# Products of the identity issued on TensorE ahead of its waits in the layer norms, the routing and the start of the feed-forward

## What is computed

```python
def first_block(...):
    for l in range(DEPTH):
        mix = hybrid_mixer(x, w_in[l], ...)
        x = layer_norm(ALPHA * x + mix, ln1_g[l], ln1_b[l])
        ffn = grouped_moe(x, router_w, router_bias, w_gate[l], w_up[l], w_down[l])
        x = layer_norm(ALPHA * x + ffn, ln2_g[l], ln2_b[l])
    return x

def second_block(x, ...):
    h = x
    for layer in range(DEPTH):
        mix = hgrn2_mixer(h, ...) if layer < N_A_LAYERS else swa_sink_mixer(h, k_shared, v_shared, ...)
        h = layer_norm_2(ALPHA_2 * h + mix, ln_mix_g[layer], ln_mix_b[layer])
        ff = conv_ffn(h, ffn_w_in[layer], ffn_conv_w[layer], ffn_conv_b[layer], ffn_w_out[layer])
        h = layer_norm_2(ALPHA_2 * h + ff, ln_ffn_g[layer], ln_ffn_b[layer])
        if layer == N_A_LAYERS - 1:
            k_flat, v_flat = jnp.split(h @ shared_w_kv, 2, axis=-1)
    return h
```

## Time and profile before

| | |
|---|---|
| median of three runs | 1679.57 us |
| the profiled execution | 1681.4 us |
| its span in the trace | 1679.6 us |
| TensorE busy | 1480.0 us |
| VectorE busy | 610.1 us |
| ScalarE busy | 463.4 us |
| GpSimd busy | 120.1 us |
| granted clock of TensorE, mean | 0.934 |

### The profile page before, as it was taken

How to read it: one execution, slowest core, us unless ns; L and a number is a source line. 1 busy time by engine, 2 the same in 40 slices (tenths; PEclk the granted TensorE clock), 3 DMA queues, 4 the chain that set the end, 5 groups by cost and what they waited for, 6 DMA issues and landing times.

```text
span 1679.6 us, 20234 instructions
## 1 busy us (share of the span) xinstructions
PE 1480.0 (88%) x7774; PEld 962.5 (57%) x7774; DVE 610.1 (36%) x1231; ACT 463.4 (28%) x866; POOL 120.1 (7%) x135
## 2 busy tenths in 40 slices
PE   6978699999699778999987897797999896899997
PEld 3854543433276444343426886367994384499943
DVE  0253311111213532011106597328770335477702
ACT  1251111110123412111104332044750035167500
POOL 1011000000000300000002151003000003000000
PEclk9999799999799889999997998869999898899999
DMA  9420499999916036999996421246564440255630
GB/s 328 152 100 1 159 392 394 397 392 393 334 52 248 1 128 224 397 392 393 397 383 199 153 89 63 83 153 195 171 232 145 136 171 1 87 189 172 228 125 25
DMA packets 184814, 347.45 MB, mean 207 GB/s; under 512 B 8208, under 2 KB 84262, under 8 KB 184628
## 3 DMA queue, kind: packets, MB, share of 16 engines
q1 hardware_dynamic: 179920, 330.19, 55.1%
q0 software_dynamic: 3968, 15.84, 2.6%
q10 hardware_dynamic: 868, 0.63, 0.1%
HBM read 342.44 MB, written 4.19 MB: 206 GB/s over the span
## 4 chain that ended last, share of the span: by engine, by line
PE 74%; SPq 9%; DVE 8%; DMA 3%; ACT 3%; issue 2%; POOL 0%; DVEq 0%; ACTq 0%
PE bank L1444 16%; SPq L575 9%; PE bank L1875 9%; PE bank L1643 8%; PE bank L1760 7%; PE bank L1761 7%; PE bank L1762 7%; PE bank L1653 5%; PE bank L1664 3%; PE bank L1704 3%; DMA slot<-in_w_down 2%; PE bank L1792 2%; PE bank L1886 1%; ACT arena L745 1%; DVE w_low L1363 1%
## 5 line engine op out<-in xcount | busy, mean ns | idle before, releaser
L1760 PE MATMUL bank<-x_high,w_high 128*128 128x256 f32 x912 | 264.0, 289 | 18.7 <-DVE w_low L1363 14.1
L1761 PE MATMUL bank<-x_low,w_high 128*128 128x256 f32 x912 | 262.9, 288 | 0.0
L1762 PE MATMUL bank<-x_high,w_low 128*128 128x256 f32 x912 | 262.7, 288 | 0.0
L1643 PE MATMUL bank<-slot,arena 128*64 128x512 f32 x1024 | 223.9, 594 | 1.6 <-DMA slot<-in_w_up 1.3
L708 ACT ACTIVATE arena<-bank 128x512 f32<-128x512 f32 (+7 forms) x196 | 99.3, 533 | 371.7 <-PE bank L1653 122.6
L1760 PEld LDWEIGHTS bank<-x_high,w_high 128*128 128x128 f32 x912 | 180.4, 198 | 20.2 <-DVE w_low L1363 14.8
L1761 PEld LDWEIGHTS bank<-x_low,w_high 128*128 128x128 f32 x912 | 180.3, 198 | 0.0
L1762 PEld LDWEIGHTS bank<-x_high,w_low 128*128 128x128 f32 x912 | 180.1, 197 | 0.0
L708 ACT ACTIVATE w_high<-slot 128x1024 fp32r<-128x1024 f32 x130 | 129.9, 1051 | 118.4 <-PE bank L1762 89.3
L1643 PEld LDWEIGHTS bank<-slot,arena 128*64 128x64 f32 x1024 | 72.4, 137 | 149.9 <-issue 149.9
L1875 PE MATMUL bank<-slot,arena 128*128 128x512 f32 x352 | 151.4, 592 | 0.0
(11 more groups left out here) (252 smaller groups left out, 1700.3 us busy)
## 6 DMA issues: line engine op xcount, KB each, us to landing
slot<-in_w_gate SPq DMA_DIRECT2D x64, 1024.0 KB, 14.0
slot<-in_w_up SPq DMA_DIRECT2D x64, 1024.0 KB, 14.2
slot<-in_w_down SPq DMA_DIRECT2D x64, 1024.0 KB, 13.9
slot<-in_ffn_w_in SPq DMA_DIRECT2D x44, 1024.0 KB, 7.5
slot<-in_ffn_w_out SPq DMA_DIRECT2D x22, 1024.0 KB, 5.0
slot<-in_hgrn_w_in SPq DMA_DIRECT2D x16, 1024.0 KB, 6.1
slot<-in_w_in SPq DMA_DIRECT2D x10, 1024.0 KB, 11.2
slot<-in_w_o SPq DMA_DIRECT2D x8, 1024.0 KB, 7.1
```

The lines of the kernel that those rows point to most:

```text
L1643: last = mm(banks_gu["gu".index(m)][rows, :], B["xe"][:, 4 * half + c, rows], ws[e][:, c, :], start=(half == 0 and c == 0), stop=(half == ...
L1760: mm(dst, high[:, k, :], x_high[:, k, :], start=(k == 0), stop=False)
L1761: mm(dst, high[:, k, :], x_low[:, k, :], start=False, stop=False)
L1762: last = mm(dst, low[:, k, :], x_high[:, k, :], start=False, stop=(k == KD - 1))
```

## The change

A function `busy(b, n)` issues n float32 products of the identity (128x128) with the identity repeated four times (128x512) into a bank. Nobody reads them, and no semaphore is raised. Each later job starts its bank anew. It is called

- in transpose_x for all calls but "in", ahead of the wait for the tile: 8 products ahead of tile 1, and ahead of tile 0 12 for the names "m" and "z", none for "y". `reuse` of the first bank comes ahead of them;
- in route ahead of the wait for `chosen_ready`: 8;
- in experts ahead of the wait for `slots_ready`: 7;
- in feed_forward ahead of the wait for the convolution's weights: 3, and behind their transposes, ahead of the first product: 5.

```diff
+            def busy(b, n):
+
+                for _ in range(n):
+                    mm(b[:, :], ident[:, :], ident[:, :].unsqueeze(1).to_broadcast([P, 4, P]), start=True, stop=True)
+
             def transpose_x(l, y, ready):
                 for t in range(NT):
+                    if y != "in":
+                        busy(reuse(pe, (l, f"{y}xT{t}0")), (8 if t else 12 if y in "mz" else 0))
                     ready(t)
...
                 b = reuse(pe, (l, "rank"))
+                busy(b, 8)
                 pe.wait_ge(sem("chosen_ready"), l + 1)
...
+                busy(reuse(pe, (l, "G0"), 0), 7)
                 pe.wait_ge(sem("slots_ready"), 2 * l + 1)
                 tokens(0)
...
             def feed_forward(l):
                 b = reuse(pe, (l, "cw"))
+                busy(b, 3)
                 pe.wait_ge(sem("cw_in"), 48 * (l - 1))
                 for i in range(2):
                     last = nc.tensor.transpose(b[:, 88 * i:88 * (i + 1)], F["cw_rows"][0:88, i, :], ident[0:88, 0:88])
                 done(last, (l, "cw"))
+                busy(reuse(pe, (l, "U00"), 0), 5)
```

## The result

The changed kernel takes 1740.45 us (median of four runs, 1738.24 to 1742.48) against 1680.22 for the kernel before in the same measurement: a ratio of 1.036, with a 95% interval of 1.0342 to 1.0379. It is slower by 60 us, where I forecast 42.7. The profiled execution took 1739.75 us with a span of 1738.0, which is 58.4 more than the span before.

What follows compares the result with a forecast made beforehand. TensorE, busy 88% of the span, was taken to bound the kernel. Site terms 3.6 + 5.0 + 3.6 + 6.6 + 3.5 + 15.6 + 4.8 = 42.7 us on 1681.4 gave 1724.1, less 1.8: 1722.3, range 1706 to 1742.

Steps and rivals of the forecast that it cites:

- The price of a product: Each unread float32 product costs 0.866 us at full clock, from the output projection, and 1.736 us at the low clock.
- The two routings: First norm and routing, layers 0 and 1: trains overrun their gaps, part given back by the clock; experts start +3.6 each.
- The norms behind the experts: Layers 0 and 1: twelve and eight products delay tile 1's transposes by 8.3 us; after clock gains +5.0 and +6.6.
- Norm z: Twelve products start only after the wait for z11, with no gap to fill, then eight more: +15.6 us.
- The feed-forwards: Norm y and feed-forward, layers 2 and 3: trains delay the first products, clock gives part back: +3.5 and +4.8 us.
- The clock holds everywhere: Rival, chance 0.14: routing trains and bias products run at full clock; cost 28 us instead of 43, total 1707.
- The clock doesn't hold: Rival, chance 0.09: transposes, narrow products and waits let the clock fall; 21 us counted as given back go, total 1744.
- A product costs one record: Rival, chance 0.05: an unread product takes 0.433 us, as the repeated identity might be cheaper; -13 us, total 1667.
- The rule weighed: Skill's warm-up rule puts TensorE at full clock in router records and bias products; forecast followed the disagreeing rows instead.

Runs made afterwards that it cites:

- kernel of a quarter of the price: Changed kernel, same places and counts, each unread product reading the identity's bytes as bf16 in one pass; 1676.99 us in one run.
- Without the branch: Changed kernel without TensorE's part of the overflow rounds (reading of the count and branch behind the experts); 1725.72 us.
- one train more: Kernel with trains cut to their gaps (1671.31 us), plus seven products ahead of layer 2's bias products; 1663.54 us, ratio 0.9885 to the kernel before.
- the routing's trains alone: Kernel before with only the routing's trains, 5 products ahead of the choice and 4 ahead of the slots; 1680.78 us, ratio 0.9991.

## Why the prediction was right, and where it was short

The direction, the mechanism and most of the sizes were right. The range held the result near its upper end.

- **The price of a product**: 0.866 us foreseen, eight in 6.87 measured. The kernel of a quarter of the price shows that it is this length and not the number that costs.
- **The two routings**: +3.6 each, measured +3.8 and +3.9. Inside them the logits took 5.17 us where I took 4.0, the eight behind them 8.83 where I had 8.9, and the gather 3.57 where I had 3.8.
- **The norms behind the experts**: the term that was mis-sized, +5.0 and +6.6 against +12.9 and +14.1. The step that failed is "TensorE ends at 445.46 and reads the count of rounds; VectorE, which reads it too, is idle for 1.4 of that window's 6.35, so at most that". I bounded one engine by another. VectorE goes on within 1.4 us, and TensorE stood 6.0 us between its last product and the train. In that time the clock fell, so the train took 13.04 us instead of 10.4. The late start (5.5 over what I took) and the slower train (2.6) make up the 7.9 missing in layer 0. Counted from the last product, tile 1's transposes started 16 us later than in the kernel before (26.8 against 10.6), where I had foreseen 8. Without the branch both are gone, and the sites cost 4.2 and 6.4, close to my steps. That the 6.0 us are a fetch of the instructions behind the branch is likely and not shown: one packet of instructions fewer for each branch speaks for it, and the kernel of a quarter of the price, in which the same branch cost at most 0.15 us, rules out the reading of the count. Why the branch is cheap there stays open.
- **Norm z**: +15.6 against +16.0. That a wait for a bank stood ahead of the train came from the planner's order and not from a row alone. TensorE idled its 5.2 us as before.
- **The feed-forwards**: +3.5 and +4.8 against +4.7 and +4.5. The DMA of the bias products took 6.29 us instead of 5.29 and added 0.8 that I had not counted. The split that stood beside GpSimd's addition hid little.
- **The rivals**: "The clock holds everywhere" is refuted by the bias products at 0.50 in the changed kernel and by their fall while TensorE was busy, in the kernel with a train ahead of them. "The clock doesn't hold" is half true: it fell in the logits and behind norm z, but rose again in each train that found it low. "A product costs one record" is refuted by the 6.87 us.
- **The rule weighed**: by the Trainium skill ("TensorE: Matmul & The Clock Gate", Part 1) the warm-up is an amount of time and not a number of matmuls. For the 32-row products the traces don't agree. 20.81 us of them at half clock, and a fall amid 16.07 us of them, decide against it here. I also took it too far when I let it put TensorE at full clock in all of the two stretches: it says so only of what comes after the warm-up.

## What to carry to other kernels

Work that only keeps an engine busy can't be broken off, so it must be shorter than its gap at the clock at which it starts, or give back what it stands over. Measured against the price of the real shape, the same idea turns from 60 us slower to 12 us faster, and to 17 with one train more, of which some 4 us are only where the clock fell. Before a wait is filled, ask what else lies under it: a bank, a branch, a fetch. And don't bound one engine's share of it by what another engine shows.

## What was unexpected of the hardware

- A branch over the code of the overflow rounds, with the reading of a count ahead of it, held TensorE for 6.0 and 6.3 us until its next instruction. With 10.3 us of work given to it ahead of the branch it cost nothing. In the kernel with products of a quarter of the price the same branch cost 0.15 us and nothing.
- Products with 32 rows, back to back, did not hold the clock: started at full clock, they ran at 0.65 in the mean and at half at their end, and started at half clock, they stayed at 0.50 for all of their 20.81 us.
- In kernels that differ only elsewhere the same code took up to 3.0 us more or less by where the clock fell (layer 3 from the projection to the down product, 170.62 us with the routing's trains alone against 167.61). The executions of the changed and the new kernels lie within 3 to 6 us of each other, those of the kernel before within 10 to 12 in the later measurements. A gain under some 5 us from one trace of such a kernel is not yet one.
